# RWKV scan: the k products in the other half of TensorE's array, the values' directions exchanged, a weight block's split and a bias addition in GpSimd's queue

## The chip, the cores and the metric

The kernel runs on one core of a Trainium2 chip. Its time is the device time of that core in microseconds (us), the median of repeated runs. One further execution was taken by the hardware profiler; the engines are named TensorE (PE, with PEld for its weight loads), VectorE (DVE), ScalarE (ACT), GpSimd (POOL) and SyncE (SP, which issues the DMAs).

## What is computed

The kernel computes a chain of network blocks. The change lies in one of them, a bidirectional RWKV mixer. Per head of 64 channels it runs a linear recurrence over 768 tokens (256 of context, 512 of the sequence) in both directions:

```python
RWKV_HEAD = 64
...
def _wkv_step(S, inp):
    r_t, w_t, k_t, v_t, a_t, b_t = inp
    sa = jnp.einsum('zbhvk,zbhk->zbhv', S, a_t)
    S = S * w_t[..., None, :] + sa[..., :, None] * b_t[..., None, :] + v_t[..., :, None] * k_t[..., None, :]
    return S, jnp.einsum('zbhvk,zbhk->zbhv', S, r_t)

def wkv_bidir(state0, scan_in):
    state, ys = lax.scan(_wkv_step, state0, scan_in)
    ys = jnp.moveaxis(ys, 0, 2)
    return state, ys[0] + ys[1][:, ::-1]
```

z is the direction, h one of 16 heads. Afterwards y is normalised per head, gets a bias and a bonus (a per-token scalar times the values v), is gated and multiplied by an output weight of 1024x1024.

## The kernel before

The scan works in chunks of 64 tokens (`CH`), 12 of them (`STEPS`), 4 of context (`CSTEPS`) and 8 of the sequence (`lat`). The two directions lie in the two halves of the 128 partitions: `lo` (0 to 63) is forward, `hi` (64 to 127) backward. Every product is therefore a pair of 64x64 products, one per half, and the helper `mmul` (L3960) issues both: rows `lo` of the array into output partitions `lo`, then `hi` into `hi`. The helper `turned` (L3975) does the same. Two quadrants of the array are used this way. `to_rows` (L3969) puts an output row of the forward direction i and of the backward direction 7 - i into the partitions of that row's parity, so for odd i its two products cross over into the other two quadrants.

The engines run their own queues in program order, tied by semaphores. For every head h of 16, TensorE's queue holds, with `walk` = h - 1 and `ahead` = h + 1:

- the products stage, called A below. `pair_set(i)` multiplies b (`bh`) and k (`kh`) by a and r (`at_rt`) for all chunks, five sets in two banks; VectorE masks each (`mask`, L3875 and L3878), scales the strict part (`scale`, L3883), adds the identity (`add_eye`, L3889) and transposes (`turn`, L3895). `turn(g)` multiplies b and k by a diagonal (`eed`), and ScalarE copies the result to `bkT` (L3774). Between these stand the first ten parts of the previous head's walk.
- the solve stage, called B below. A triangular system is inverted in 5 levels of 3 groups, 15 steps n: `grow_z(n)` on TensorE, a copy to `Z` on ScalarE (L3797), a second product, an addition to `R` and a transpose on VectorE (L3941, L3895). `off` comes from GpSimd (L3708). Between these stand the other 26 parts of the walk (`WALK_PARTS`) and, for the head ahead, its factors: exponentials on ScalarE (L3746 to L3759), products on VectorE (L3832 to L3864) and GpSimd (L3687 `km`, L3692 `kh`, L3694 `eed`).

The walk carries the state over the chunks. Each chunk j has three parts on TensorE with a ScalarE copy after each: `walk_state` (x = pairs times v, plus a times state; also the value and decay terms of the state's change `ds_psum`), `walk_solve` (sa = R times x, and output rows), `walk_share` (the sa term of ds and of the output rows). The last head's walk runs in the next stage, `walk_finish`, beside the output projection.

VectorE's queue has, between stages A and B, three more operations of the head: `add_bonus` (L3917), `split_block` (L3928: the low part of one 128x512 block of the output weight, raw minus rounded) and `add_shift` (L3923: the bias row added to the bonus rows). SyncE waits for the split to store both parts, then loads the next block, and behind that loads the factors of the head after next.

## Time and profile before

| | us |
|---|---|
| median of 3 runs | 4052.1 |
| lowest and highest | 4043.2 to 4055.37 |
| span of the profiled execution | 4039.7 |
| scan, heads 1 to 15 with their walks (2847.3 to 3398.5 of the span) | 551.2 |

The profile is one execution; its durations are of that one. A timeline row gives the start and duration of a run of like instructions in us, engine, line, operation, output and inputs, shape, count, and in brackets the idle time ahead and what ended it. A float32 product of the program appears as two instructions (passes).

### The profile page before, as it was taken

The page shows a single profiled execution, that of the slowest core. Times are in us where ns is not written, and L with a number is a line of the kernel's source. Part 1 is how long each engine was busy: PE and PEld are TensorE (multiplying, and loading weights), DVE is VectorE, ACT ScalarE, POOL GpSimd, SP SyncE. Part 2 cuts the span into 40 slices and gives each one's busy share as a digit, 9 for nine tenths or more (in the row PEclk, how much of TensorE's full clock was granted, in tenths as well). Part 3 has the DMA queues.
Part 4 walks back from the last instruction along what each step waited for, and adds up shares of the span by engine and source line. Part 5 has one row for each costly group of instructions (what it writes and reads, how often), then busy time and mean ns, then how long its engine had stood idle before and what let it go on. Part 6 is the DMA issues. An engine that isn't in the chain of part 4 may idle for free. (4 is left out here: it accounts for less than half of the span.)

```text
span 4039.7 us, 81581 instructions
## 1 busy us (share of the span) xinstructions
PE 3727.0 (92%) x32706; PEld 2683.2 (66%) x32706; DVE 2360.8 (58%) x3864; ACT 1204.0 (30%) x2668; POOL 1321.7 (33%) x1020
## 2 busy tenths in 40 slices
PE   8888999898999999899999997998999999899887
PEld 6667878657787898777344444874999998733333
DVE  4568882545985445565444445767888776623333
ACT  3352222344222322331111112224455454111112
POOL 4443444434445364573000000431555453000000
PEclk9999999999999999999999999999999999899999
DMA  4114542303554122345999995356333234589997
GB/s 128 56 53 170 184 157 93 104 1 105 178 187 146 66 96 75 99 138 228 404 420 420 420 420 212 134 177 201 88 89 91 78 93 147 199 366 422 421 421 316
DMA packets 231204, 787.80 MB, mean 195 GB/s; under 512 B 56008, under 2 KB 64024, under 8 KB 171136
## 3 DMA queue, kind: packets, MB, share of 16 engines
q1 hardware_dynamic: 225008, 764.12, 50.9%
q0 software_dynamic: 5328, 19.40, 1.2%
q8 instruction: 219, 3.59, 0.4%
q14 instruction: 73, 0.60, 0.0%
q10 hardware_dynamic: 576, 0.09, 0.0%
HBM read 736.15 MB, written 47.38 MB: 194 GB/s over the span
## 5 line engine op out<-in xcount | busy, mean ns | idle before, releaser
L2887 POOL DMA_INDIRECT moe0e_xg<-moe_h,moe_first_rows x20 | 18.9, 947 | 546.3 <-DVE moe_first_rows L3044 540.5
L3011 ACT ACT_TABLE_LOAD x32 | 41.1, 1283 | 519.2 <-PE moe1e_p_u L2957 262.4
L373 POOL TENSOR_TENSOR gmi_w_lo<-gmi_rows_w,gmi_w_hi 128x512 fp32r<-128x512 f32 x64 | 120.2, 1878 | 159.8 <-ACT gmi_w_hi L415 159.8
L3960 PE MATMUL scan_bank<-scan_T,scan_off 64*64 64x64 f32 x3840 | 159.4, 220 | 8.5 <-issue 5.7
L373 POOL TENSOR_TENSOR p_w_lo<-p_rows_w,p_w_hi 128x512 fp32r<-128x512 f32 (+3 forms) x88 | 113.5, 1291 | 159.9 <-ACT p_w_hi L415 159.9
L2887 POOL DMA_INDIRECT moe1e_xg<-moe_h,moe_first_rows x17 | 16.0, 940 | 451.0 <-DVE moe_first_rows L3044 444.4
L1159 POOL TENSOR_TENSOR f0u_w_lo<-f0u_w,f0u_w_hi 128x1024 fp32r<-128x1024 f32 x42 | 115.0, 2757 | 137.6 <-ACT f0u_w_hi L1175 137.6
L1159 POOL TENSOR_TENSOR f1u_w_lo<-f1u_w,f1u_w_hi 128x1024 fp32r<-128x1024 f32 x42 | 114.3, 2742 | 137.5 <-ACT f1u_w_hi L1175 137.5
L1227 DVE SCALAR_TENSOR_TENSOR f0u_ada<-hT,condition,f0u_ada 128x512 f32<-128x512 f32 x168 | 148.2, 949 | 16.4 <-DMA hT<-in_ada_w_dram 15.9
L1227 DVE SCALAR_TENSOR_TENSOR f1u_ada<-hT,condition,f1u_ada 128x512 f32<-128x512 f32 x168 | 140.5, 903 | 20.5 <-DMA hT<-in_ada_w_dram 20.0
L2984 PE MATMUL moe0e_p_y<-moe_ring,moe0e_gatedT 128*64 128x512 f32 x608 | 137.6, 605 | 7.8 <-ACT moe0e_gatedT L3013 7.8
L3960 PEld LDWEIGHTS scan_bank<-scan_T,scan_off 64*64 64x64 f32 x3840 | 137.2, 135 | 10.5 <-issue 6.8
L373 POOL TENSOR_TENSOR rp_w_lo<-rp_rows_w,rp_w_hi 128x512 fp32r<-128x512 f32 x48 | 79.9, 1666 | 164.8 <-ACT rp_w_hi L415 164.8
L2984 PE MATMUL moe1e_p_y<-moe_ring,moe1e_gatedT 128*64 128x512 f32 x512 | 113.4, 595 | 10.8 <-DVE x L3040 9.4
L3797 ACT ACTIVATE scan_Z<-scan_bank 128x256 f32<-128x256 f32 x240 | 91.4, 381 | 97.1 <-PE scan_bank L3960 95.8
L3960 PE MATMUL scan_bank<-walk_memory 64*64 64x64 f32 x1708 | 116.0, 222 | 4.3 <-issue 1.7
L2957 PE MATMUL moe0e_p_g<-gm_uT,moe0e_xT 128*64 128x512 f32 x444 | 118.1, 600 | 0.8 <-ACT moe0e_xT L3005 0.8
L2957 PE MATMUL moe0e_p_u<-gm_uT,moe0e_xT 128*64 128x512 f32 x444 | 116.2, 592 | 0.0
L440 DVE CAST gmi_x_hi<-hT 128x768 fp32r<-128x768 f32 x64 | 42.9, 670 | 125.2 <-PE gmi_bank L362 124.9
L2984 PEld LDWEIGHTS moe0e_p_y<-moe_ring,moe0e_gatedT 128*64 128x64 f32 x608 | 50.0, 139 | 86.8 <-issue 71.3
L3708 POOL TENSOR_TENSOR scan_off<-scan_pairs,scan_join 128x256 f32<-128x256 f32 x120 | 101.3, 880 | 0.0
L3708 POOL TENSOR_TENSOR scan_off<-walk_memory,scan_join 128x256 f32<-128x256 f32 x120 | 100.4, 873 | 0.0
(903 smaller groups left out, 11529.7 us busy)
## 6 DMA issues: line engine op xcount, KB each, us to landing
moe_ring<-in_moe_w_down_dram SPq DMA_DIRECT2D x140, 1024.0 KB, 18.0
gm_uT<-in_moe_w_gu_dram SPq DMA_DIRECT2D x111, 1024.0 KB, 16.6
moe_ring<-in_moe_w_gu_dram SPq DMA_DIRECT2D x102, 1024.0 KB, 24.7
walk_memory<-in_moe_w_gu_dram SPq DMA_DIRECT2D x60, 1024.0 KB, 24.4
hT<-in_ada_w_dram SPq DMA_DIRECT2D x48, 1024.0 KB, 6.8
f0u_w<-in_ffn_w_gate_up_dram SPq DMA_DIRECT2D x22, 1024.0 KB, 4.8
f1u_w<-in_ffn_w_gate_up_dram SPq DMA_DIRECT2D x22, 1024.0 KB, 4.8
gmi_rows_w<-in_ga_w_in_dram SPq DMA_DIRECT2D x64, 256.0 KB, 2.7
```

The costliest lines, as they stand in the source:

```text
L373: nc.gpsimd.tensor_tensor(w_lo[t % 2][:, 0:width], w[t % RAW][:, 0:width], w_hi[t % 2][:, 0:width], ALU.subtract).then_inc(w_lo_made, 1)
L440: nc.vector.tensor_copy(x_hi[t % 2][:, tok], hT[:, k, tok]).then_inc(x_hi_made, 1)
L1159: nc.gpsimd.tensor_tensor(w_lo[u][:, g], w[:, g], w_hi[u][:, g], ALU.subtract).then_inc(lo_made, 1)
L1227: ins = V.scalar_tensor_tensor(out=acc[:, z, :], in0=src, scalar=cond[:, n * HALF + k, z:z + 1], in1=acc[:, z, :], op0=ALU.mult, op1=ALU.add)
L2887: pool.indirect_dma_start(xg[:], None, H.h, bass.IndirectOffsetOnAxis(rows[:, 0:1], 0)).then_inc(gathered, 16)
L2957: mm = nc.tensor.matmul(p[r, :], xT[:, kd, r], weights(s, half, second)[:, k, g * HID:(g + 1) * HID], start=(kd == 0), stop=(kd == KD - 1) ...
L2984: mm = nc.tensor.matmul(p_y[n][r, :], aT[:, kh, r], ring[s, half][:, k, n * BANK:(n + 1) * BANK], start=(kh == 0), stop=(kh == KH - 1), sk ...
L3011: nc.scalar.activation(sg[:], p_g[:], ACT.Silu).then_inc(silu_ready, 1)
L3708: nc.gpsimd.tensor_tensor(off[n][:], strict(u, g), over4(join[:, l + 1, :]), ALU.mult).then_inc(s["off_ready"], 1)
L3797: A(Z[n % 2][:], quad(z_bank[n % 2]), ACT.Copy).then_inc(s["z_copied"], 1)
L3960: mm = nc.tensor.matmul(out[r], lhsT[r], rhs[r], start=start, stop=stop, skip_group_check=True)
```

## The change

In the scan and in `walk_finish`:

- k's products (pairs and turned copies) go through a new helper `crossed`: rows `hi` of the array into output partitions `lo`, rows `lo` into `hi`. b's products stay. They are interleaved, b and k into different banks, in three groups instead of five sets (`BPAIR_BANK`, `KPAIR_BANK`, `TURN_BANK`), and b and k are masked apart.
- Everything that is made of k's pairs and turned copies then lies in the exchanged halves, so the values v are loaded with their directions exchanged, their masks too, and the products with v (x, state, output rows) cross over.
- Two row halves of the array now add to the same partitions of a bank, so four semaphores order them: `xv_done`, `dsv_done`, `yr_done`, `yv_done`. The x product of the values moves from `walk_state(j)` to the end of `walk_share(j - 1)`, that of the output rows too; the decay term moves from `walk_state` to `walk_solve`.
- `split_block` and `add_shift` leave VectorE's queue for GpSimd's: they stand behind the next head's `kh` and ahead of its `eed`.
- GpSimd makes `R` and the first level of `off` in turns; ScalarE's copies of turned groups stand one place earlier among the walk's copies.
- In `walk_finish`, `walk_share` issues the state's product ahead of the output row's.

```diff
+    BPAIR_BANK, KPAIR_BANK = (0, 2, 4), (1, 3, 0)
+    TURN_BANK = (1, 3, 1)
...
-                    for z, rows in ((0, lo), (1, hi)):
+                    for z, rows in ((0, hi), (1, lo)):
                         sp.dma_start(vs[h % 2][rows, :, :], vS[z].rearrange("s t c -> t s c")[:, :, h * HK:h * HK + HK]).then_inc(v_loaded[h % 2], 16)
...
+                def split_block(h):
+                    pool.wait_ge(s["hi_made"], h + 1)
+                    nc.gpsimd.tensor_tensor(w_lo[:], w_raw[:], w_hi[:], ALU.subtract).then_inc(s["lo_made"], 1)
...
                     nc.gpsimd.tensor_tensor(kh[:], cs(km), cs(e_neg), ALU.mult).then_inc(s["kh_made"], 1)
+                    if h:
+                        split_block(h - 1)
+                        add_shift(h - 1)
                     pool.wait_ge(s["bd_ready"], h + 1)
...
-                    mask(0)
+                    mask_b(0)
                     scale(0)
-                    mask(1)
-                    mask(2)
+                    mask_k(0)
+                    mask_b(1)
                     scale(1)
-                    mask(3)
-                    mask(4)
+                    add_eye(0)
+                    mask_b(2)
                     scale(2)
-                    add_eye(0)
+                    mask_k(1)
                     add_eye(1)
+                    mask_k(2)
                     add_eye(2)
...
                     add_bonus()
-                    split_block()
-                    add_shift()
...
+                def crossed(out, lhsT, rhs, start=True, stop=True):
+
+                    for r, o in ((hi, lo), (lo, hi)):
+                        mm = nc.tensor.matmul(out[o], lhsT[r], rhs[r], start=start, stop=stop, skip_group_check=True)
                     return mm
...
                     else:
-                        mmul(x_psum, pairs[u][:, j, 2, :], vs[u][:, j, :], stop=False)
+                        pe.wait_ge(s["xv_done"], w * (STEPS - 1) + j)
                         pe.wait_ge(s["sm_ready"], w * (STEPS - 1) + j)
                         mmul(x_psum, at(w, j), Sm[:], start=False).then_inc(s["x_ready"], 1)
-                    if 0 < j < STEPS - 1:
-                        mmul(ds_psum, bkT[u][:, j, 1, :], vs[u][:, j, :], stop=False)
-                        mmul(ds_psum, eed[w % 3][:, j, :], Sm[:], start=False, stop=False)
+                    if j < STEPS - 1:
+                        crossed(ds_psum, bkT[u][:, j, 1, :], vs[u][:, j, :], stop=False).then_inc(s["dsv_done"], 1)
...
+                    if j < STEPS - 1:
+                        values_to_x(w, j + 1).then_inc(s["xv_done"], 1)
+                        if i >= -1:
+                            if i == -1 and w:
+                                pe.wait_ge(s["y_copied"], w)
+                            values_to_rows(i + 1, pairs[u][:, j + 1, 3, :], vs[u][:, j + 1, :], start=i == -1).then_inc(s["yv_done"], 1)
...
+                        if g == 1:
+                            pe.wait_ge(s["kpairs_masked"], h * NG + 2)
+                            pe.wait_ge(s["bpairs_masked"], h * NG + 3)
...
+                            mm_b = mmul(bank[TURN_BANK[g]][:, o], bh[:, j, :], eed[h % 3][:, j, :])
+                            mm_k = crossed(bank[TURN_BANK[g] + 1][:, o], kh[:, j, :], eed[h % 3][:, j, :])
```

How this moves instructions, at two places. First TensorE's queue in stage A of head 1, from the walk's third step (state) on; `scan_eed` with `scan_bh` or `scan_kh` are the turned copies, `scan_v, scan_pairs` x of the values, `scan_v, scan_bkT` their state term. Before:

```order
L3960 MATMUL scan_bank5<-scan_v0,scan_pairs0 64x64 x2
L3960 MATMUL scan_bank5<-walk_memory 64x64 x2
L3960 MATMUL scan_bank6<-scan_v0,scan_bkT0 64x64 x2
L3960 MATMUL scan_bank6<-walk_memory 64x64 x2
L3975 MATMUL scan_bank3<-scan_eed1,scan_bh 64x64 x2
L3975 MATMUL scan_bank3<-scan_eed1,scan_kh 64x64 x2
```

After, where turn(1) stands ahead of that step (L3971 is `mmul`, L3986 `crossed`):

```order
L3971 MATMUL scan_bank<-walk_memory,scan_bkT0 64x64 x2
L3986 MATMUL scan_bank<-scan_v0,scan_pairs0 64x64 x2
L3971 MATMUL scan_bank<-scan_eed1,scan_bh 64x64 x2
L3986 MATMUL scan_bank<-scan_eed1,scan_kh 64x64 x2
...
L3971 MATMUL scan_bank<-walk_memory 64x64 x2
L3986 MATMUL scan_bank<-scan_v0,scan_bkT0 64x64 x2
```

The k products are issued right behind b's, now into other quadrants; turn(1) has moved ahead of the walk's third step, and x of the values into the step before.

Second, GpSimd's queue from one head's solve to the next, before:

```order
L3703 TENSOR_TENSOR scan_R<-scan_pairs,scan_join 128x256 x3
L3708 TENSOR_TENSOR scan_off<-scan_pairs,scan_join 128x256 x15
L3687 TENSOR_TENSOR scan_km<-head_memory,scan_t 128x768
L3692 TENSOR_TENSOR scan_kh<-scan_km,scan_e_neg 128x768
L3694 TENSOR_TENSOR scan_eed<-scan_eye,scan_ee 128x704
```

And after:

```order
L3717 TENSOR_TENSOR scan_R<-scan_pairs,scan_join 128x256
L3720 TENSOR_TENSOR scan_off<-scan_pairs,scan_join 128x256 x13
L3696 TENSOR_TENSOR scan_km<-head_memory,scan_t 128x768
L3701 TENSOR_TENSOR scan_kh<-scan_km,scan_e_neg 128x768
L3683 TENSOR_TENSOR scan_w_lo<-scan_w_raw,scan_w_hi 128x512
L3688 TENSOR_TENSOR rw_y_bonus<-rw_y_bonus,scan_shift 128x4x64
L3706 TENSOR_TENSOR scan_eed<-scan_eye,scan_ee 128x704
```

The two operations that left VectorE stand between `kh` and `eed`, behind all of `off`.

## Rows read from the trace of the kernel before

**Rows 1.** The page: its first line, and TensorE's busy time.

```profile
span 4039.7 us, 81581 instructions
...
PE 3727.0 (92%) x32706; PEld 2683.2 (66%) x32706; DVE 2360.8 (58%) x3864; ACT 1204.0 (30%) x2668; POOL 1321.7 (33%) x1020
```

**Rows 2.** Busy time by stretches: head 10's stages A and B, heads 1 to 15.

```profile
core 0: us, PE busy (x) PEld busy (x) DVE busy (x) ACT busy (x) POOL busy (x), PEclk, DMA share, GB/s
3180.41:3190.85 10.44, 10.44 (x304) 10.41 (x300) 8.44 (x17) 4.29 (x14) 4.96 (x7) 1.00 0.18 43
3190.85:3217.63 26.78, 25.36 (x826) 24.12 (x824) 21.47 (x44) 14.98 (x48) 15.06 (x15) 1.00 0.36 104
2847.30:3398.50 551.20, 529.50 (x16572) 510.50 (x16568) 439.51 (x886) 283.44 (x895) 294.26 (x312) 1.00 0.29 80
```

**Rows 3.** Timeline, TensorE in stage A: pair products, then turned copies.

```profile
3185.01 0.42 PE L3960 MATMUL scan_bank<-scan_at_rt,scan_bh 64*64 64x128 f32 x4
...
3185.45 0.41 PE L3960 MATMUL scan_bank<-scan_at_rt,scan_bh 64*64 64x128 f32 x4
...
3186.12 0.31 PE L3975 MATMUL scan_bank<-scan_eed,scan_kh 64*64 64x64 f32 x4
...
3186.35 0.31 PE L3975 MATMUL scan_bank<-scan_eed,scan_kh 64*64 64x64 f32 x4
```

**Rows 4.** Timeline, TensorE where crossed (L3969) and straight products meet.

```profile
3062.17 0.22 PE L3969 MATMUL scan_bank<-walk_memory,scan_at_rt 64*64 64x64 f32 x1
3062.18 0.22 PE L3960 MATMUL scan_bank<-walk_memory 64*64 64x64 f32 x1
3062.18 0.22 PE L3969 MATMUL scan_bank<-walk_memory,scan_at_rt 64*64 64x64 f32 x1
3062.18 0.22 PE L3960 MATMUL scan_bank<-scan_T,scan_off 64*64 64x64 f32 x1
3062.23 0.22 PE L3969 MATMUL scan_bank<-walk_memory 64*64 64x64 f32 x1
```

**Rows 5.** Timeline, VectorE in stage A and at the start of B.

```profile
3182.53 0.42 DVE L3883 TENSOR_TENSOR scan_pairs<-scan_pairs,scan_w 128x256 f32<-128x256 f32 x1
...
3182.88 0.68 DVE L3878 TENSOR_TENSOR scan_pairs<-scan_bank,scan_masks 128x512 f32<-128x512 f32 x1
...
3187.64 0.45 DVE L3895 STREAM_TRANSPOSE scan_T<-scan_R 128x256 f32<-128x256 f32 x1
...
3191.80 1.11 DVE L3928 TENSOR_TENSOR scan_w_lo<-scan_w_raw,scan_w_hi 128x512 fp32r<-128x512 f32 x1
...
3192.83 0.94 DVE L3923 TENSOR_TENSOR rw_y_bonus<-rw_y_bonus,scan_shift 128x256 f32<-128x256 f32 x1
```

**Rows 6.** Timeline: ScalarE's copy of a turned group, then one hop of the walk.

```profile
3187.17 0.60 ACT L3774 ACTIVATE scan_bkT<-scan_bank 128x512 f32<-128x512 f32 x1 [0.19 <-PE scan_bank L3975]
...
3196.41 0.22 ACT L3727 ACTIVATE walk_memory<-scan_bank 128x64 f32<-128x64 f32 x1
3196.69 0.27 PE L3960 MATMUL scan_bank<-walk_memory 64*64 64x64 f32 x2
...
3197.07 0.31 ACT L3731 ACTIVATE walk_memory<-scan_bank,walk_memory 128x64 f32<-128x64 f32 x1 [0.43 <-PE scan_bank L3960]
```

**Rows 7.** Timeline, second part of B: a transpose and the product behind it.

```profile
3208.63 0.45 DVE L3895 STREAM_TRANSPOSE scan_T<-scan_R 128x256 f32<-128x256 f32 x1
...
3209.19 0.68 PE L3960 MATMUL scan_bank<-scan_T,scan_off 64*64 64x64 f32 x16 [0.74 <-issue]
```

**Rows 8.** Timeline, B: VectorE's two-input operation beside GpSimd's off, then km.

```profile
3199.28 0.96 DVE L3837 SCALAR_TENSOR_TENSOR scan_at_rt<-head_memory,scan_negkk,scan_e_exc 128x384 f32<-128x384 f32 x1
...
3200.79 1.80 POOL L3687 TENSOR_TENSOR scan_km<-head_memory,scan_t 128x768 f32<-128x768 f32 x1
...
3200.97 2.04 DVE L3837 SCALAR_TENSOR_TENSOR scan_at_rt<-head_memory,scan_negkk,scan_e_exc 128x384 f32<-128x384 f32 x1
```

**Rows 9.** The page's groups: a 128x512 split on GpSimd in another stage.

```profile
L373 POOL TENSOR_TENSOR gmi_w_lo<-gmi_rows_w,gmi_w_hi 128x512 fp32r<-128x512 f32 x64 | 120.2, 1878 | 159.8 <-ACT gmi_w_hi L415 159.8
```

**Rows 10.** Timeline, TensorE in B: products with one column.

```profile
3202.30 1.51 PE L3960 MATMUL scan_bank<-ones,scan_sq 64*64 64x1 f32 x48
```

More of the change, by code:

```diff
@@ L3580, in rwkv_scan @@
         rk = sb("rk", [P, lat, CH])
-        bank = [st.ps(f"bank{n}", [P, BANK]) for n in range(8)]
+        banks = st.ps("bank", [P, 8, BANK])
+        bank = [banks[:, n, :] for n in range(8)]
         W4 = 4 * CH
-        pair_bank, tr_bank = bank[0:2], bank[2:5]
         z_bank, zr_bank = (bank[0][:, 0:W4], bank[1][:, 0:W4]), (bank[2][:, 0:W4], bank[3][:, 0:W4])
@@ L4008, in walk_share @@
+                    if 0 < j < STEPS - 1:
+                        mmul(ds_psum, eed[w % 3][:, j, :], Sm[:], start=False, stop=False)
+                    if i >= 0:
+                        to_rows(i, rt(w, j), Sm[:]).then_inc(s["yr_done"], 1)
                 def walk_share(w, j):
                     u = w % 2
+                    i = j - CSTEPS
+                    if i >= 0:
+                        pe.wait_ge(s["yr_done"], w * lat + i + 1)
                     pe.wait_ge(s["sa_copied"], w * STEPS + j + 1)
@@ L4148, in rwkv_tables @@
     incl = halves(early | same, early.T | same)
+    strict_of_values, incl_of_values = halves(early.T, early), halves(early.T | same, early | same)
     joins = []
@@ L4217, in walk_finish @@
         logit_bank = [bank[5 + t % 2][:, 0:36] for t in range(NT)]
-        x_ready, x_copied, sa_ready, sa_copied, ds_ready, sm_ready, y_ready, y_copied = (walk.sems[n] for n in WALK_SEMS)
-        walked, shared = LAST * STEPS, LAST * (STEPS - 1)
+        x_ready, x_copied, sa_ready, sa_copied, ds_ready, sm_ready, y_ready, y_copied, xv_done, dsv_done, yr_done, yv_done = (walk.sems[n] for n in WALK_SEMS)
+        walked, shared, rowed = LAST * STEPS, LAST * (STEPS - 1), LAST * lat
         consts_loaded, row_loaded, route_loaded = (st.sem(n) for n in ("consts_loaded", "row_loaded", "route_loaded"))
@@ L4296, in walk_state, with values_to_x @@
+                def values_to_x(j):
+                    return crossed(x_psum, walk.pairs[:, j, 2, :], walk.v[:, j, :], stop=j == 0)
                 def walk_state(j):
-                    v = walk.v[:, j, :]
                     if j == 0:
-                        mmul(x_psum, walk.pairs[:, j, 2, :], v).then_inc(x_ready, 1)
-                        mmul(ds_psum, walk.bkT[:, j, 1, :], v, stop=False)
+                        values_to_x(j).then_inc(x_ready, 1)
                     else:
-                        mmul(x_psum, walk.pairs[:, j, 2, :], v, stop=False)
+                        pe.wait_ge(xv_done, shared + j)
@@ L4303, in walk_state, with walk_solve @@
                         pe.wait_ge(sm_ready, shared + j)
                         mmul(x_psum, walk.at_rt[:, 0, j, :], walk.Sm[:], start=False).then_inc(x_ready, 1)
+                    if j < STEPS - 1:
+                        crossed(ds_psum, walk.bkT[:, j, 1, :], walk.v[:, j, :], stop=False).then_inc(dsv_done, 1)
+                def walk_solve(j):
+                    i = j - CSTEPS
+                    if i >= 0:
+                        pe.wait_ge(yv_done, rowed + i + 1)
+                        to_rows(i, walk.at_rt[:, 1, j, :], walk.Sm[:]).then_inc(yr_done, 1)
+                    if j < STEPS - 1:
+                        pe.wait_ge(dsv_done, shared + j + 1)
@@ L4323, in walk_share @@
                     if j < STEPS - 1:
-                        mmul(ds_psum, walk.bkT[:, j, 0, :], walk.SA[:], start=False).then_inc(ds_ready, 1)
+                        values_to_x(j + 1).then_inc(xv_done, 1)
+                        if i >= -1:
+                            values_to_rows(i + 1, walk.pairs[:, j + 1, 3, :], walk.v[:, j + 1, :], start=i == -1).then_inc(yv_done, 1)
                 def turn_o(t, h):
```

211 lines of the change are left out of this document (112 added, 99 removed).

## The prediction

> **What bounds the kernel now.** I read the page first: one core, a span of 4039.7 us, TensorE busy 92% of it [rows 1]. The change touches only the RWKV scan and the last head's walk behind it, so the next view was busy time by stretches [rows 2]. The scan's fifteen heads that carry a walk take 551.2 us together, 36.75 us each. For head 10 I cut that at its first solve product: 10.44 us in which the pair products and the turned copies are made (stage A), and 26.78 us in which the triangular solve runs (stage B). The granted clock is 1.00 in all three stretches, the 2.4 GHz level, so the clock is no lever here. In stage A TensorE is busy all 10.44 us and VectorE 8.44; in B TensorE 25.36 and VectorE 21.47. TensorE sets A. B is shared: its solve chain and the walk's chain both go through TensorE's one queue.
>
> Next came the rates, in the timeline of TensorE [rows 3]. A float32 product of the program is two passes, and each row groups four instructions (two passes in each half of the array). With 64 columns two rows are 0.23 us apart, so a pass takes 0.0291 us of the queue; with 128 columns two rows are 0.44 us apart, 0.0545 us a pass. The two halves alternate, so a single quadrant takes a pass every 0.058 us. The trace already holds places where the other two quadrants are fed too, because the products for the output rows (L3969) cross over when their row is odd [rows 4]: four starts lie within 0.01 us, and the next four come 0.06 us later. That is four passes in the time of two.
>
> **Part 1, k products across (pairs and turned copies).** Per head they are 32 passes of 64 columns and 64 of 128 for the pairs, 88 of 64 for the turned copies: 120 x 0.0291 + 64 x 0.0545 = 6.98 us, all of it in stage A. Half of them move to the unused quadrants, interleaved with the b products, so by [rows 4] the queue time halves: -3.49 us. The walk's value products in A (x and state, four steps) save at most 8 x 0.117 = 0.9 us; I take 0.5. TensorE would need 10.44 - 3.5 - 0.5 = 6.45 us.
>
> What is late next is VectorE. Its masks, scales and identity additions feed the banks that the turned copies are written to: turn(1) now waits for the k pairs of group 1 to be masked. From the stage's start: 0.23 us to the pairs (their row starts at 3180.64, the stage at 3180.41), 0.47 + 0.3 for the first group at the new rate and its tail, then by [rows 5] mask b0, scale, mask k0 at 0.42 each (256 elements; I take the scale's row), mask b1 0.69, scale 0.42, identity addition and transpose 0.87 (the addition, 256 elements too, at 0.42), mask b2 0.69, scale 0.42, mask k1 0.69: 5.04 us. So turn(1) starts at 6.0. The walk's third step stands behind it, and ScalarE's copy of the turned group now lies ahead of that step's x copy. A hop of the walk I read as 0.38 us from TensorE's start to ScalarE's, 0.22 or 0.31 us of copy and 0.06 us back [rows 6]: 0.69 us on average. So: turned products 0.47, to the copy 0.35, the copy 0.60, x copy and back 0.28, two more hops 1.38, the state's products 0.12, in all 9.2, and 0.1 for GpSimd's port (below): the first solve product at 9.3. **A is 1.1 us shorter**, not 4. Bounds: 0, if GpSimd holds VectorE up at each of its six scales and additions, to 2.8, if only the walk's nine hops and two ScalarE copies of 0.6 between them count (6.2 + 1.2, and 0.23 at the start).
>
> **Part 2, the walk's values in stage B.** A step j of 4 to 11 has 18 products in pairs of halves, 9 pairs of 0.117 us. After the change x, state and row values cross over; straight and crossed split 6 to 3 for even rows and 5 to 4 for odd ones. Odd rows had 3 crossed already. So a step needs 0.70 us instead of 1.05, or 0.58 instead of 0.70: 4 x 0.35 + 4 x 0.12 = 1.9 us less work in B. Not all of it is time: B holds 26 walk parts and so 26 x 0.69 = 17.9 us of hops, and ScalarE does 15 copies of the solve and five activations over 768 elements between them. TensorE stands idle in B for such a copy (in [rows 6] its products start 0.06 us behind the copy's end) and for VectorE's transpose ([rows 7]: 0.74 us, ended 0.11 us behind the transpose). I take 1.5 of the 1.9, port costs of part 3 included; bounds 0 and 3 (with part 3's gain).
>
> The new waits of TensorE on itself (xv_done, dsv_done, yr_done, yv_done) protect sums to which two row halves add. They are 11 + 11 + 8 + 8 = 38 in a head. Each is counted up one part ahead of its wait, and the same part waits for a ScalarE copy that can only start after it: nothing, as long as that copy is the later one; without that cover each would cost the tail of a product, 0.3 us. Queued behind them is the whole of TensorE's queue.
>
> **Part 3, block split and bias addition from VectorE to GpSimd.** VectorE loses 1.11 + 0.94 = 2.05 us [rows 5], which stand directly ahead of its first addition of B. TensorE then waits on walk copies, not on VectorE, so most of this is slack: inside the 1.5 above. On GpSimd they come after kh and ahead of eed, where it waits for VectorE's last factors, the 13th of 15 slots of B, anyway. Price: no row has this split on GpSimd in the scan; another stage's same size is 1.88 us [rows 9], and by the km row (1.80 us for 768 elements [rows 8]) 1.2; the addition is 0.6 by km, 0.94 if it takes VectorE's time. It delays eed by 2.8 us at most, and eed is first needed by turn(0) of the next head. SyncE's queue is passed too: its stores of the split block, and behind them the next loads, start when GpSimd is done, some 13 us later in the head (from 3192.9 [rows 5] to km's end at 3202.6 [rows 8] with kh and the split behind it), but the loads held up are for two heads ahead. Both at nothing.
>
> What I do charge is the port. While GpSimd works on km, VectorE's operation with two SBUF inputs takes 2.04 us in place of 0.96, and ends only 0.4 us after km has [rows 8]. The same would befall VectorE once or twice in a head behind kh: 0 to 2.8 us, taken as 1.0, and half of it hidden: 0.5, already taken off in the 1.5. The Trainium skill ("SBUF — State Buffer", section "SBUF: two separate sides") says the pair of ports is locked for a whole instruction and the loser fully blocks; this trace agrees, and by that rule moving element-wise work to GpSimd hides none of it where VectorE is busy.
>
> **Sum.** A head gains 1.1 + 1.5 = 2.6 us; 15 heads 39. The first head has no walk to wait for: VectorE's part, 2 us. The last walk, outside the scan: each share now sends the state product ahead of the row products, 7 x 0.117 = 0.8, taken as 1. Together 42 us. The profiled span of 4039.7 lies 12.4 us under the median of the runs, 4052.1; I put the difference on top: 4052.1 - 42 = **4010 us**.
>
> **Rivals.**
> 1. TensorE's gain is kept in full, because the order of VectorE's queue leaves turn(1) less late than I say: A 2.8 us shorter, B 2.6. 15 x 5.4 = 81, and 1 for the last walk: 3970. For it: TensorE alone fills A today. Against: VectorE's 8.44 us in A, the walk's hops. Chance 0.12.
> 2. TensorE's queue has a least price per pass that no quadrant lifts. For it: products of one column go at 1.51 us for 48, tail included, 0.028 us each, no faster than 64 columns [rows 10]. Then the 64-column passes gain nothing, the 128-column ones halve (-1.75 us), TensorE needs 8.7 us in A and the forecast's chain ends at 9.5; B gains only by VectorE's start: 1.2 us a head, 18 in all and 1 for the last walk, 4033. Against it: the four starts within 0.01 us [rows 4]; by those the one-column products are held to 0.058 us a quadrant too. Chance 0.10. The Trainium skill ("TensorE: Matmul & The Clock Gate", section "Back-to-back issue gap") has such a floor of about 25 ns per small product; with it A's work would fall by 2.4 us instead of 3.5 (184 passes at 25 ns for 6.98 us). The trace speaks against it.
> 3. The change does not bring its parallel run where it stands: the crossed products read the same rows as the straight ones, and queue behind them. A 0.3 shorter, B 0.3: 4043, no difference. Chance 0.10.
> 4. Slower: GpSimd's split and addition catch VectorE in the second part of B, where TensorE already waits for transposes ([rows 7]: 0.74 us). Both caught in full cost 2.8 us a head; with A unchanged and 1.3 us of B's saving left, that is 1.5 us x 15 = 22: 4074. It decides from the point at which the waiting of VectorE exceeds what A and the walk give, 1.3 us. Chance 0.08.
>
> **How the numbers follow.** The forecast, 4010 with its own range of 3988 to 4034, has 0.60. The range for all of it runs from 3978 to 4044: it holds the forecast, rival 2, rival 3 and the near edge of rival 1. A measurement of this kernel tells about 0.3% from no change, 12 us. Faster by more than that (under 4040): forecast 0.60, rival 1 0.12, rival 2 0.10, in all 0.82; within it: rival 3, 0.10; slower 0.08.
>
> **What the profile of the changed kernel would show.** Right: rows of the pair products at half their spacing, stage A at 9.3 us with VectorE nearly full and TensorE with gaps ahead of turn(1); heads 34 us apart; GpSimd's split right behind kh. Wrong: pair products still 0.22 us apart (rival 3), A at 7 (rival 1), two-input operations of VectorE over 1.5 us behind kh and solve products waiting for transposes (rival 4). If heads differ in nothing but the last walk does, the sum's places are wrong.

## The result, and the profile after

The changed kernel is slower: 4116.4 us, the median of 4 runs (4100.4 to 4125.8), where the kernel before ran beside it in 4049.2 us (4 runs, 4043.2 to 4055.4). The ratio is 1.0166, 95% interval 1.0139 to 1.0194: 67 us more, where I had forecast 42 less and a range up to 4044.

The page of the profile after: span and busy times, and the granted clock in 40 slices.

```profile
span 4112.3 us, 82090 instructions
...
PE 3710.4 (90%) x32706; PEld 2649.4 (64%) x32706; DVE 2346.9 (57%) x3848; ACT 1202.6 (29%) x2668; POOL 1337.8 (33%) x1052
...
PEclk9999999999999999999999999998989898999999
```

Against [rows 1] TensorE has the same 32706 products and is busy 16.6 us less, in a span that is 72.6 us longer. 70 of the 72.6 lie in the scan's heads 1 to 15. Busy time by stretches, as in [rows 2]: head 10's stage A, its stage B, heads 1 to 15, and last 6.83 us out of head 10:

```profile
core 0: us, PE busy (x) PEld busy (x) DVE busy (x) ACT busy (x) POOL busy (x), PEclk, DMA share, GB/s
3223.44:3234.44 11.00, 7.89 (x289) 7.02 (x281) 9.77 (x19) 4.10 (x13) 8.48 (x12) 0.87 0.18 41
3234.44:3266.74 32.30, 27.15 (x843) 25.84 (x843) 17.85 (x40) 14.90 (x47) 12.53 (x13) 0.89 0.32 86
2848.40:3469.60 621.20, 510.04 (x16566) 478.45 (x16558) 405.22 (x871) 280.73 (x895) 310.76 (x342) 0.92 0.27 71
...
3231.62:3238.45 6.83, 5.80 (x136) 5.64 (x138) 2.66 (x6) 2.83 (x12) 6.83 (x10) 0.50 0.02 6
```

A head takes 41.4 us in place of 36.75. TensorE does work less (510 us for 529.5), VectorE too, and all of them wait more. The clock, 1.00 throughout in [rows 2], is 0.92 on average: there are stretches at half, the 1.2 GHz level, as the last row shows.

What TensorE waited for in the scan, before and then after (us in total, times, longest; each over its own fifteen heads):

```profile
PE scan_bank L3960 <- issue: 12.3, 20, 1.2
PE scan_bank L3969 <- issue: 3.0, 3, 1.5
PE scan_bank L3960 <- ACT walk_memory L3727: 2.0, 11, 0.2
```

```profile
PE scan_bank L3971 <- issue: 53.5, 54, 3.9
PE scan_bank L3986 <- issue: 13.3, 14, 2.0
PE scan_bank L3971 <- ACT walk_memory L3751: 11.8, 30, 0.8
PE scan_bank L3971 <- ACT walk_memory L3742: 11.4, 32, 0.5
PE scan_bank L3980 <- issue: 5.8, 5, 2.3
```

Two things grew: waits for ScalarE's copies of the walk, and "issue", stretches in which TensorE stood idle and no engine and no transfer of the program ended it. One of the latter, in stage A of head 10 (the answer to [rows 3]):

```profile
3224.67 0.28 PE L3971 MATMUL scan_bank<-scan_at_rt,scan_bh 64*64 64x128 f32 x2
3224.68 0.27 PE L3986 MATMUL scan_bank<-scan_at_rt,scan_kh 64*64 64x128 f32 x2
3224.78 0.28 PE L3971 MATMUL scan_bank<-scan_at_rt,scan_bh 64*64 64x128 f32 x2
...
3226.41 0.27 PE L3986 MATMUL scan_bank<-scan_at_rt,scan_kh 64*64 64x128 f32 x1 [1.25 <-issue]
```

Four passes (two b, two k) every 0.11 us: 0.028 us each against 0.0545 before, the rate that I had forecast. But in the middle of the group, with no wait in the program, TensorE stands for 1.5 us from start to start.

### The profile page after: what moved, and what is told of

The parts are those of the page before. It is cut to its first block and busy times, and to the rows that moved or that the text cites. A ratio compares the mean times of both kernels' runs of the same rounds, so it can differ in the third digit from the quotient of the medians.

```text
span 4112.3 us, 82090 instructions
## 1 busy us (share of the span) xinstructions
PE 3710.4 (90%) x32706; PEld 2649.4 (64%) x32706; DVE 2346.9 (57%) x3848; ACT 1202.6 (29%) x2668; POOL 1337.8 (33%) x1052
## 5 line engine op out<-in xcount | busy, mean ns | idle before, releaser
L3971 PE MATMUL scan_bank<-scan_T,scan_off 64*64 64x64 f32 x3840 | 185.0, 237 | 23.6 <-issue 22.7
L1227 DVE SCALAR_TENSOR_TENSOR f0u_ada<-hT,condition,f0u_ada 128x512 f32<-128x512 f32 x168 | 199.0, 1253 | 0.4 <-DVE f0u_ada L1227 0.4
L3971 PEld LDWEIGHTS scan_bank<-scan_T,scan_off 64*64 64x64 f32 x3840 | 160.0, 151 | 25.7 <-issue 24.2
L3952 DVE TENSOR_TENSOR walk_memory<-walk_memory,scan_bank 128x256 f32<-128x256 f32 x120 | 50.3, 419 | 106.5 <-PE scan_bank L3971 105.9
L3952 DVE TENSOR_TENSOR scan_R<-scan_R,scan_bank 128x256 f32<-128x256 f32 x120 | 50.2, 418 | 96.8 <-PE scan_bank L3971 96.4
L3971 PE MATMUL scan_bank<-walk_memory 64*64 64x64 f32 x1064 | 88.8, 241 | 17.3 <-ACT walk_memory L3742 5.2
## 6 DMA issues: line engine op xcount, KB each, us to landing
moe_ring<-in_moe_w_gu_dram SPq DMA_DIRECT2D x102, 1024.0 KB, 24.3
```

The costliest lines, as they stand in the source:

```text
L1227: ins = V.scalar_tensor_tensor(out=acc[:, z, :], in0=src, scalar=cond[:, n * HALF + k, z:z + 1], in1=acc[:, z, :], op0=ALU.mult, op1=ALU.add)
L3952: V.tensor_tensor(R[u][:, g4, :], R[u][:, g4, :], quad(zr_bank[n % 2]), ALU.add).then_inc(s["zr_added"], 1)
L3971: mm = nc.tensor.matmul(out[r], lhsT[r], rhs[r], start=start, stop=stop, skip_group_check=True)
```

## Experiments

Each was timed beside the kernel before (medians of 4041.1 to 4042.2 us in these runs; the changed kernel's ratio puts it at 4109 there). "A" and "B" are the two stages as means over heads 1 to 15, cut in each trace at the first solve product and the last one of the head. "Stops" are distances of over 0.2 us between two neighbouring products of one group and line with no wait between them, in us a head beyond the usual distance.

### Which wait is attached

In the trace a product on TensorE (its weight load) carries one wait, the one called first; what is called behind it stands in instructions of their own, of mostly 51 ns and with up to two waits in one. In the scan there are 494 of these before and 929 after. After the change the *first called* are the waits of TensorE on itself, and those that fell out are the copy waits on which it really waits (x_copied, sm_ready, sa_copied: 420 of the 929).

```diff
-                        pe.wait_ge(s["xv_done"], w * (STEPS - 1) + j)
                         pe.wait_ge(s["sm_ready"], w * (STEPS - 1) + j)
+                        pe.wait_ge(s["xv_done"], w * (STEPS - 1) + j)
...
-                    if i >= 0:
-                        pe.wait_ge(s["yr_done"], w * lat + i + 1)
                     pe.wait_ge(s["sa_copied"], w * STEPS + j + 1)
+                    if i >= 0:
+                        pe.wait_ge(s["yr_done"], w * lat + i + 1)
```

> The changed kernel with one edit: at the three places of the walk where TensorE waits for itself (xv_done, yv_done, yr_done) and for a ScalarE copy, the two waits are called in the other order, so that the copy wait is attached to the product and the self wait, long satisfied, is the instruction of its own. Same instructions, same count. Theory W (a copy wait on an instruction of its own lengthens the hop from ScalarE's copy to TensorE's start, in the traces from 0.05 to 0.14 us, some 36 hops a head): 0.09 x 36 x 15 = 49 us come back, 4066 to 4075. Theory S (TensorE is starved of instructions because it runs through them faster: stops inside groups without a wait grew from 1.2 to 4.3 us a head): nothing comes back, 4105 to 4118. Both at once: 4075 to 4095.

Measured: 4082.5 us, ratio 1.0105 (1.0080 to 1.0131). 25 us come back by exchanging the order of two calls. The hop from ScalarE's copy to TensorE, timeline of the changed kernel and then of this one:

```profile
3241.37 0.22 ACT L3742 ACTIVATE walk_memory<-scan_bank 128x64 f32<-128x64 f32 x1
...
3241.74 0.27 PE L3971 MATMUL scan_bank<-walk_memory 64*64 64x64 f32 x2 [0.33 <-ACT walk_memory L3742]
```

```profile
3215.76 0.22 ACT L3751 ACTIVATE walk_memory<-scan_bank 128x64 f32<-128x64 f32 x1
...
3216.04 0.27 PE L3971 MATMUL scan_bank<-walk_memory 64*64 64x64 f32 x2
```

The product starts 0.15 us behind the copy's end in the one, 0.06 in the other, which is what [rows 6] had. Not all of the 49 us of theory W came, since not all hops were longer: of the walk's 540 hops in the scan 175 start 0.14 to 0.16 us behind their copy in the changed kernel, 3 in this one. At 0.09 us each that is 15 of the 25 us; the rest was not traced. The self waits were also not "long satisfied": 214 of the 285 for x and for the output rows (xv_done, yr_done) came true less than 0.06 us ahead of the wait instruction, so the queue stood at them.

The reverse on the kernel before, with a wait that has been true since the first head:

```diff
+                    pe.wait_ge(s["at_ready"], 1)
                     pe.wait_ge(s["x_copied"], w * STEPS + j + 1)
```

> The kernel before with one edit: ahead of each of the walk's three copy waits on TensorE stands a wait that has been satisfied since the first head, so that the copy wait becomes an instruction of its own; 36 more instructions a head, nothing crossed. Theory W: the hop grows by 0.09 us here too, 36 x 15 x 0.09 = 49 us at most, 4080 to 4098, with the stops inside groups as before. Theory S: 36 more among some 1100 instructions a head, a third of a fetch, under 3 us in all: 4049 to 4055.

Measured: 4094.5 us, 1.0132 (1.0115 to 1.0149). And the same wait called behind the copy wait:

> The kernel before with the same satisfied waits as in waits_apart (4094), called behind the copy waits, so that the copy wait stays attached to its product and the satisfied one is the instruction of its own: the same 36 instructions more a head. If what costs is where the copy wait sits: 4042 to 4056, at most 0.3 us a head for the instructions themselves. If it is the number of instructions: 4080 to 4098 again.

Measured: 4057.9 us, 1.0038 (1.0025 to 1.0050). The edits add 35 waits a head, in the trace 510 instructions in fifteen heads. So waits that are already true cost 16 us, 0.03 us each, and the place of the copy wait another 37. Theory W has the size, but its "stops inside groups as before" is wrong: they rise from 1.2 us a head to 1.9 in waits_ahead and 3.0 in waits_apart, 10 of the 16 us and 27 of the 52. Longer hops (139 in waits_apart, 3 before) account for 12. These stops too end where a block of instructions has come in (24 of 28 of over 1 us, 2.3 to 2.9 us behind its start); why more wait instructions bring more of them, no run shows. Still, my step "nothing, as long as that copy is the later one" is shown wrong on an unchanged kernel.

### Split and addition on GpSimd

```diff
                     add_bonus()
-                    split_block()
-                    add_shift()
...
                     nc.gpsimd.tensor_tensor(kh[:], cs(km), cs(e_neg), ALU.mult).then_inc(s["kh_made"], 1)
+                    if h:
+                        split_block(h - 1)
+                        add_shift(h - 1)
```

> The kernel before with only the output weight's split and the bias addition moved to GpSimd, behind kh. My prediction had VectorE freed of 2.05 us a head and a port price of 1.0, in all a gain of 0 to 1 us a head: 4034 to 4050. If GpSimd's share of the port is the cause of the slowdown: 1 us a head or more lost, 4065 to 4085.

Measured: 4073.8 us, 1.0070 (1.0053 to 1.0087): 32 us lost by a move costed at a small gain. VectorE is not what suffers. Its groups of factors before, and then with the move:

```profile
L3843 DVE TENSOR_TENSOR scan_bh<-scan_ka,scan_e_neg 128x384 f32<-128x384 f32 x28 | 26.2, 935 | 0.0
L3837 DVE SCALAR_TENSOR_TENSOR scan_at_rt<-head_memory,scan_negkk,scan_e_exc 128x384 f32<-128x384 f32 x18 | 25.9, 1440 | 0.0
```

```profile
L3859 DVE TENSOR_TENSOR scan_bh<-scan_ka,scan_e_neg 128x384 f32<-128x384 f32 x28 | 31.4, 1121 | 0.0
L3853 DVE SCALAR_TENSOR_TENSOR scan_at_rt<-head_memory,scan_negkk,scan_e_exc 128x384 f32<-128x384 f32 x18 | 20.9, 1160 | 0.0
```

One is 5 us longer in sum, the other 5 shorter: other operations meet GpSimd's, no more of them. What moved is SyncE's queue. Head 10 starts at 3180.6 before and at 3204.3 with the move; its transfers in the two:

```profile
3192.93 0.33 SPq L3656 DMA_DIRECT2D rw_wo_hi<-scan_w_hi  x1
...
3198.64 1.11 SPq L3527 DMA_DIRECT2D head_memory<-rw_a  x2
3201.49 3.40 SPq L3534 DMA_DIRECT2D head_memory<-rw_cum  x4
3209.41 1.08 SPq L3527 DMA_DIRECT2D head_memory<-rw_k  x2
3214.91 1.08 SPq L3527 DMA_DIRECT2D head_memory<-rw_r  x2
```

```profile
3229.32 0.33 SPq L3656 DMA_DIRECT2D rw_wo_hi<-scan_w_hi  x1
...
3231.42 1.12 SPq L3527 DMA_DIRECT2D head_memory<-rw_a  x2
3232.58 3.24 SPq L3534 DMA_DIRECT2D head_memory<-rw_cum  x4
3235.92 1.17 SPq L3527 DMA_DIRECT2D head_memory<-rw_k  x2
3238.95 1.50 SPq L3527 DMA_DIRECT2D head_memory<-rw_r  x2
```

Before, they spread over 22 us; now all start 25 us into the head, within 10. GB/s in 40 slices of the scan, before and with the move:

```profile
GB/s 53 103 82 92 92 51 139 64 72 111 81 63 113 60 107 84 44 152 80 65 119 52 92 91 53 139 77 68 103 81 92 101 43 136 66 59 39 32 42 5
```

```profile
GB/s 82 64 154 5 135 83 3 206 14 86 133 3 170 48 5 185 32 23 196 3 89 128 5 149 68 4 188 32 63 154 5 138 80 5 186 31 27 66 3 41
```

What suffers is TensorE, and the traces point at its own instructions. They too come by transfers (the queue called "instruction" in the DMA view, 131 blocks of 16 KB in these 15 heads). In the trace of the move, a block whose first 2.5 us fall where over half of the DMA engines are busy is followed by 1.0 us of stop, another by 0.1 us. Over half is not enough by itself: before has 18 such blocks, with 0.07 us each. What the move adds are blocks beside over 85% of the DMA engines, 13 in place of 2, with 1.5 us each. To test that without GpSimd:

```diff
+                    if ahead is not None:
+                        sp.wait_ge(s["kh_made"], h + 2)
                     sp.wait_ge(s["lo_made"], h + 1)
```

> The kernel before with one edit, on SyncE alone: its stores of the split block, and with them the loads queued behind, wait for kh of the next head, so they start some 12 us later in the head (in the trace of before the stores start 12.3 us into head 10; with the split on GpSimd 25.0 us) and come without gaps between them. No instruction of any other engine is moved; VectorE keeps split and addition. Theory D (transfers in one burst hold up TensorE's instruction fetches; in the trace with the move to GpSimd a fetch whose first 2.5 us lie beside transfers on over half of the DMA engines is followed by 1.0 us of stop inside a group, another by 0.1 us): the 30 us of that move come here too, 4060 to 4075 where before is 4042. Theory P (GpSimd works longer and takes the port from VectorE): nothing changes, 4036 to 4050.

Measured: 4064.0 us, 1.0058 (1.0038 to 1.0079). One wait on SyncE, no work of any compute engine moved, and 22 of the 32 us are there; the stops go from 1.2 to 2.4 us a head, as with the move, and 13 blocks stand beside over 85%, with 1.5 us of stop each. And the cure, GpSimd's work as in the change but SyncE's loads of rates and decays issued ahead of the stores (load_factors takes the stores as a call between its second and third group):

> Split and bias addition on GpSimd as in pool_only (4074), with SyncE's queue put in another order: the loads of rates and decays for the head after next go ahead of the stores of the split block and the load of the next raw block; keys and reads stay behind. Theory D: the burst is spread again, most of the 30 us come back, 4036 to 4055. Theory P: 4065 to 4085.

Measured: 4049.8 us, 1.0025 (1.0015 to 1.0035), stops 1.4 us a head and 3 such blocks: 24 of the 32 us come back. The 8 that stay were not traced further.

### How fast TensorE gets instructions

Four runs of products were added once, ahead of the first head:

```diff
+ for wide, count in ((CH, 256), (2 * CH, 128)):
+     for quads in (1, 0):
+         for q in range(count):
+             mmul(bank[1][:, 0:wide], sq[:, 0:CH], sq[:, 0:wide])
+             if quads:
+                 for r, o in ((hi, lo), (lo, hi)):
+                     mm = nc.tensor.matmul(bank[2][o, 0:wide], sq[r, 0:CH], sq[r, 0:wide], start=True, stop=True, skip_group_check=True)
+             else:
+                 mm = mmul(bank[1][:, 0:wide], sq[:, 0:CH], sq[:, 0:wide])
...
```

> The kernel before, with four runs of float32 products added once, ahead of the first head's sums on TensorE (they write banks that nothing reads): 2048 passes of 64 columns on four quadrants, 2048 of 64 columns straight, 1024 of 128 columns on four quadrants, 1024 of 128 columns straight, each run waited for before the next. By the rate of my prediction (four quadrants take four passes in the time of two) they last 30, 60, 28 and 56 us. Theory S (instruction blocks of 16 KB, about 124 passes each, were never fetched less than 3.3 us apart in any trace so far, so a pass costs at least 0.027 us however many quadrants run): 55, 60, 28 and 56 us, so that 64 columns gain nearly nothing and 128 columns halve.

Busy time of the four runs (64 columns on four quadrants, 64 straight, 128 on four quadrants, 128 straight), in one execution:

```profile
2797.60:2858.40 60.80, 34.92 (x2050) 32.62 (x2048) 0.61 (x2) 0.94 (x2) 3.60 (x2) 0.97 0.26 50
2858.40:2920.20 61.80, 60.72 (x2052) 60.15 (x2048) 0.00 (x0) 0.00 (x0) 0.00 (x0) 1.00 0.02 4
2920.20:2949.30 29.10, 28.72 (x1025) 27.99 (x1024) 0.00 (x0) 0.00 (x0) 0.00 (x0) 1.00 0.02 5
2949.30:3005.40 56.10, 56.04 (x1025) 55.87 (x1024) 0.00 (x0) 0.00 (x0) 0.00 (x0) 1.00 0.01 2
```

This is the clearest view of the study. With 64 columns four quadrants take 60.8 us for what two take 61.8: no gain. TensorE is busy 35 of the 60.8 and stands still for the rest; one period of the pattern:

```profile
2836.95 0.22 PE L3960 MATMUL scan_bank<-scan_sq 64*64 64x64 f32 x2
2836.96 0.26 PE L3986 MATMUL scan_bank<-scan_sq 64*64 64x64 f32 x2
...
2838.61 0.27 PE L3986 MATMUL scan_bank<-scan_sq 64*64 64x64 f32 x1 [1.38 <-issue]
```

128 passes at 0.015 us each, then 1.6 to 1.9 us of stop, and again, 15 times (the first two stops, beside the last loads, are 4.0 and 2.5 us). The DMA view has 16 blocks of instructions for these 2048 passes, so a block carries 128, and their starts are 3.4 to 3.8 us apart, even where no other transfer runs. So over any length beyond a block a pass here costs at least 3.4 / 128 = 0.027 us. At 128 columns a straight pass costs twice that, and four quadrants bring the full factor, 29.1 for 56.1 us.

The Trainium skill ("Runtime: NRT & Kernel Launch", section "Instruction fetch mechanics") has the blocks of 16 KiB, 256 instructions, which agrees with 128 pairs of weight load and product. It also says that crossing a block's end is mostly hidden since instructions are issued slower than fetched. That nearly holds for straight products here (three stops, 1.7 us, in the 61.8), and fails for four quadrants at 64 columns.

### Crossing alone, order alone

With the split back on VectorE, what is left of the change:

> The changed kernel with the two waits in the other order (swapped, 4083) and split and bias addition back on VectorE, behind the bonus, as in before: what is left of the change is the crossing, its self waits and the order of the parts. If the costs add (30 us for the move): 4048 to 4060, within 0.3% of before, so that the crossing and its new waits cancel. If the crossing carries the gain of 42 us that I predicted once the other two costs are gone: 4000 to 4015.

Measured: 4063.8 us, 1.0052 (1.0037 to 1.0068): still slower. The changed kernel without crossing, self waits and GpSimd's work, hence its order of parts alone (diff: the crossed helpers write out[r] again, the row values stand behind the state's row product, the self waits are gone):

> The changed kernel without crossing, without the self waits and with split and addition back on VectorE: what is left is the order of the parts (pairs in three groups of their own banks, the walk's parts between them, the copies' order on ScalarE, values of x and state behind the share). If order and banks are neutral: 4034 to 4050, as before. If the order does harm of its own: 4055 or more, and crossing with its waits (swapped_dve, 4064) costs little more. If it helps: under 4030.

Measured: 4060.9 us, 1.0047 (1.0032 to 1.0063). The order does harm of its own. Its stage A is 11.35 us where before has 10.33; two waits for the walk stand in every head at the stage's end, here head 10's:

```profile
3197.83 0.45 PE L3967 MATMUL scan_bank<-walk_memory 64*64 64x64 f32 x8 [0.40 <-ACT walk_memory L3726]
...
3199.74 0.33 PE L3967 MATMUL scan_bank<-walk_memory 64*64 64x64 f32 x4 [0.53 <-ACT walk_memory L3735]
```

In the order before, a bonus (L4051) or a turned group (L3975) stands at each of these hops, and the walk's products (L3960) follow without a wait:

```profile
3188.77 0.34 PE L3960 MATMUL scan_bank<-walk_memory 64*64 64x64 f32 x4
3189.00 0.63 PE L4051 MATMUL scan_bank<-ones,scan_rk 64*64 64x1 f32 x16
3189.52 0.33 PE L3960 MATMUL scan_bank<-walk_memory 64*64 64x64 f32 x4
3189.68 0.28 PE L3975 MATMUL scan_bank<-scan_eed,scan_bh 64*64 64x64 f32 x4
```

In the new one the third step's solve has only a bonus ahead, and share and next state follow each other with nothing between. And the same order with the waits of swapped_dve but all products straight:

> swapped_dve with all crossed products straight (the row values stand behind the state's row product, with a satisfied wait in place of yv_done): order of the parts, number and place of the waits are the same, so the difference to swapped_dve (4064) is crossing alone. If costs add: order_only (4061) and 38 more waits (16 us by waits_ahead), 4072 to 4080, so that crossing is worth 8 to 16 us of the 80 that its 5.4 us less work a head would be. If crossing is worth nothing: 4058 to 4068. If it does harm: under 4055.

Measured: 4082.2 us, 1.0097 (1.0079 to 1.0114). Against swapped_dve this is crossing but for two things: the row values stand behind the state's row product instead of in the share before, and in the last walk the waits are called in the changed kernel's order. The difference is 18 us, all of what the scan shows of it in stage A (11.43 to 10.11 us; B 27.83 and 27.98). The same comparison with every other cost of the change in place:

> The changed kernel with every crossed product made straight again (k products, x, state and row values; masks and value rows as before; the row values stand behind the state's row product, as before), the order of the parts, the number of waits and GpSimd's work as in the changed kernel. If running four quadrants at once gives its 5.4 us of TensorE work a head and only waits cost time (theory W alone), this is slower than the changed kernel, 4140 to 4190. If the faster run is paid back by missing instructions (theory S), the stops inside groups fall from 4.3 back to about 1.2 us a head and the time is 4095 to 4120, no slower. Under 4090 crossing itself does harm.

Measured: 4117.5 us, 1.0183 (1.0166 to 1.0200), 8 us above the changed kernel's 4109 on this scale. The two intervals overlap (that of the changed kernel is 1.0139 to 1.0194), so here crossing is not shown to be worth anything. The stops fall only to 3.4 us a head; the burst is still there.

Then the tail of stage A was moved:

```diff
                     part(walk_share, 1)
-                    turn(1)
+                    bonus(1)
                     part(walk_state, 2)
-                    bonus(1)
+                    turn(1)
                     part(walk_solve, 2)
-                    turn(2)
                     part(walk_share, 2)
+                    turn(2)
```

> crossed_lean (4061) with the end of stage A in another order: on TensorE the second bonus ahead of the third step's state, turn(1) behind it, and turn(2) behind the third step's share instead of ahead of it; ScalarE's copies in the order that goes with it. One unfilled hop remains in place of one and a half. If the two stops at the end of stage A are what the new order costs: 0.6 us a head less, 4048 to 4054. If VectorE's masks set stage A: no change, 4056 to 4064. Faster than before only under 4030.

> order_only (4061) with the same end of stage A and without the two implied waits of lean: if the stops at the end of stage A are the cost of the order, 0.6 to 1.0 us a head and 7 us for the waits come back, 4038 to 4046; if something else in the order costs (banks, masks in eight pieces on VectorE, waits for them), 4050 to 4056.

Measured: tail 4054.4 us, 1.0034 (1.0023 to 1.0046), 6 us less than crossed_lean (4060.5, below); straight_tail 4046.8 us, 1.0013 (1.0003 to 1.0022), 14 less than order_only, 7 of which are lean's. So the tail is about 7 of the order's 19 us. The other 12 were not located; the masks in more pieces and the new bank waits are candidates that no run separates.

### A faster kernel

Since a wait that is already true costs 0.03 us, I looked for waits in the kernel before that another in TensorE's queue implies:

```diff
-                        if n >= 2:
-                            pe.wait_ge(s["z_copied"], h * NZ + n - 1)
...
-                        if n >= 2:
+                        if n == NZ - 1:
                             pe.wait_ge(s["zr_added"], h * NZ + n - 1)
```

> The kernel before without two waits of TensorE in each of the solve's 15 slots that another wait in its queue already implies: z_copied ahead of a z group (the product two slots back waited for it) and zr_added ahead of a product (t_made of the group ahead of it implies it, but for the last slot). 26 instructions of their own fewer a head. 540 satisfied waits of 36 a head cost 16 us in waits_ahead, 0.03 us each; if that holds, 390 fewer save 12 us: 4026 to 4034. If a satisfied wait costs only where TensorE is already late: 4038 to 4042.

Measured: 4035.2 us against 4042.2, ratio 0.9981 (0.9972 to 0.9990), 11 and 15 runs. The fastest of all, by 7 us. The trace has 314 wait instructions in the scan in place of 494: the second and third wait of a z group had shared one, so 12 a head are gone and not 26, and each is worth 0.04 us.

> swapped_dve (4064: crossing, copy waits attached, split and addition on VectorE) without the same two waits as in lean. If the saving is that of lean: 4050 to 4054, above before still. If the crossed kernel is held by the supply of instructions, 26 fewer of some 1100 give another 0.2 of a fetch a head, under 3 us more: 4047 to 4054 likewise. Under 4035 it would be faster than before, and crossing worth keeping.

Measured: 4060.5 us, 1.0043 (1.0027 to 1.0058), 3 us under swapped_dve, less than their intervals. No version with crossing beat the kernel before.

## Why the prediction was wrong, step by step

The runs form a chain from before to after, one part at a time:

| step (kernel) | ratio to before | us | A, B in us a head | stops in us a head |
|---|---|---|---|---|
| before | 1 | | 10.33, 26.42 | 1.2 |
| + order of the parts (order_only) | 1.0047 | +19 | 11.35, 26.57 | 1.4 |
| + 38 waits, 27 of them instructions, copy waits attached (straight_waits) | 1.0097 | +20 | 11.43, 27.83 | 2.3 |
| + crossing (swapped_dve) | 1.0052 | -18 | 10.11, 27.98 | 3.5 |
| + GpSimd's work (swapped) | 1.0105 | +21 | 10.04, 29.61 | 4.2 |
| + copy waits fall out (after) | 1.0166 | +25 | 10.30, 31.12 | 4.3 |

**What failed most: the waits, costed at nothing.** Their cover was there as I said, the copy came true later than the self wait in 385 of the 394 pairs that swapped's trace shows, and they still cost 20 us as instructions (405 in 15 heads, 0.05 us each) and 25 by taking the copy waits' place. The step looked at when a wait comes true, not at which wait the product carries, and not at the queue that has to pass it.

**Part 3: "Both at nothing."** I saw SyncE's stores start some 13 us later and asked only whether the loads come in time. They do: TensorE waits for no transfer in these traces. I did not ask what starts together with them. The port, which I charged with 0.5 to 1 us a head, was not where the 1.4 us went: the VectorE groups add up to no more than before (pool_only). Rival 4 had the sign and, by chance, the number (4074 for pool_only's 4073.8) with a mechanism that the trace does not bear out.

**Part 1, TensorE's work.** The rate from [rows 4], four passes in the time of two, is right for as long as one block of instructions lasts, and I took it for 184 passes in a row. TensorE's busy time in head 10's stage A did fall from 10.44 to 7.89 us; what came in return were stops. In stage A alone, distances of over 0.2 us ahead of a product for which no wait is called rose from 0.06 to 1.7 us a head in swapped_dve, half of the 3.49 that I had taken off (0.2 in straight_waits, so crossing brings them). An estimate from the rates run says the same: head 10's stage A has 304 passes, at 128 in 3.4 us these take 8.1 us but for what lies ready at its start, and I had put TensorE's need at 6.45. Rival 2, a least price per pass that no quadrant lifts, was the true account of the rate: 64 columns gain nothing, 128 halve. Its time, 4033, missed as the forecast did, since it had the waits and the transfers at nothing too. I gave it 0.10, because the row of four close starts spoke against it; a spacing over a few passes says nothing about a price that is levied per block. The Trainium skill's floor of about 25 ns ("TensorE: Matmul & The Clock Gate", "Back-to-back issue gap"), which I weighed there, comes near the 27 ns of sustained supply; but the rates run shows single passes at 15 ns, so here it is no floor of the single pass.

**Stage A.** I had 1.1 us less. Crossing gives 1.3 against straight_waits, close to it but not by the chain that I wrote down, which has no stops; the new order takes 1.0, and I had given it no term at all, having costed its tail as "two more hops 1.38" inside the chain without setting it against what the old order hid there.

**Part 2, stage B.** 1.5 of 1.9 us of saved work were to come. Crossing moved B by +0.15. Why none came stays open. The walk's hops are no shorter and B's blocks of instructions come no sooner, but the lower clock below also grows with crossing.

**First head and last walk.** The first head, without a walk, reaches its first solve product 8.5 us behind its first pair product in place of 10.6: the 2 us that I had. The cause that I gave, VectorE's part, is not shown: in single executions straight_waits, with the split on VectorE, has 8.2 and order_only 10.6. The changed kernel loses the 2 us again in its stage B (27.3 for 24.3). The last walk's products of TensorE take 40.9 us for 38.8, +2.1 where I had -1. They take 41.5 in order_only, which crosses nothing, so the new order is enough for that.

**The clock.** "No lever here" was a reading of before, and it did not hold for after: 6.7 us a head at the 1.2 GHz level, and 3.6 to 4.7 in the other crossed kernels, where those with straight products have 0 to 1.8. In head 10 of the changed kernel TensorE ran passes on four quadrants in bursts between stops ahead of the fall. What this costs stays open. Over heads 1 to 14 of one crossed kernel the period rises by 0.25 to 0.33 us for each us at the lower clock; at 0.3 that would be 1.1 to 1.4 us a head in the other crossed kernels and 2.0 in the changed one (an estimate; that the one causes the other is not shown). It bears on two steps of the chain: with crossing the lower clock goes from 0.7 to 3.6 us a head, which by this rate hides 13 us of what crossing gives, and from swapped to after from 4.7 to 6.7, 9 of those 25 us. No run takes it apart, and head 7 of the changed kernel has none of it and still takes 40.3 us.

## What to carry to other kernels

Before making many small instructions faster, divide the stretch's instructions by the rate at which they arrive: here 128 passes every 3.4 us, at which the straight 64-column products ran already. Do it for each stretch longer than a block, not for the whole: a head's 1105 passes would need 29 us of its 36.75, stage A's 304 need 8.1 of 10.4. Where an instruction has two waits, call first the one that comes true last, and drop waits that the queue implies. When work moves to another engine, follow its stores and the loads queued behind them, and ask what else needs the DMA engines at the new time; instruction blocks are among it.

## What the runs showed of the hardware that I had not expected

- TensorE's instruction blocks start at least 3.3 us apart in every trace, and where TensorE had stood still for over 1 us without a wait, its products resume 2.3 to 2.9 us behind a block's start: 294 of 313 such stops in the scans of all traces.
- A burst of ordinary transfers costs TensorE time without any wait in the program: 22 us by one wait on SyncE. The Trainium skill ("SBUF — State Buffer", section "SBUF: two separate sides") says that a DMA and a compute operation cannot slow each other. For the operands no run here speaks against it. But TensorE does lose time beside a burst, and its stops lie where its own instruction blocks come in beside it (1.5 us behind each of 13 blocks, with over 85% of the DMA engines busy).
- Two calls in the other order are worth 25 us (swapped), 37 us in waits_apart against waits_ahead: where the copy wait is an instruction of its own, a third of the hops (175 of 540) are 0.09 us longer. One more wait instruction costs 0.03 us where it is already true and 0.05 where it is a self wait.
